# A placement budget with longer step durations and a reserve, in a two-block transformer kernel on one core

## The reference, cut to what matters

```python
def conformer_conv(val_b, gate_b, conv_w, conv_b, ln_g, ln_b):
    g = val_b * jax.nn.sigmoid(gate_b)
    c = causal_depthwise_conv(g, conv_w)      # width CONV_W = 31
    c = c + conv_b
    c = layer_norm(c.reshape(bsz, seq, H_B, HD_B), ln_g, ln_b)   # groups of 128 channels
    return jax.nn.silu(c).reshape(bsz, seq, D_B)                 # D_B = 512

def second_block(...):
    h = rms_norm(x, norm1_g); u_a, v_a, val_b, gate_b = split(h @ w_in)
    mix = concatenate([spatial_gating(u_a, v_a, ...), conformer_conv(val_b, gate_b, ...)])
    x = x + mix @ w_out
    h = rms_norm(x, norm2_g)
    x = x + square(relu(h @ w_ff1)) @ w_ff2
    return rms_norm(x, final_g)
```

## Time and profile before

| what | value |
|---|---|
| median of 3 runs | 2759.99 us |
| the profiled execution | 2761.34 us |
| its span, first to last instruction | 2759.7 us |
| TensorE matmul busy | 2632.9 us (95%) |
| VectorE busy | 1561.2 us (57%) |
| ScalarE busy | 1060.4 us (38%) |
| mean granted TensorE clock | 0.975 |

### The profile page before, as it was taken

One profiled execution on the slowest core, in us unless ns is written; L12 is line 12 of the kernel. 1 busy time (PEld: TensorE's weight loads), 2 busy tenths in 40 slices (PEclk: granted clock), 3 DMA queues, 4 the chain that ended last, 5 costly groups with the idle time before them and its releaser, 6 DMA issues.

```text
span 2759.7 us, 33118 instructions
## 1 busy us (share of the span) xinstructions
PE 2632.9 (95%) x12696; PEld 2164.5 (78%) x12696; DVE 1561.2 (57%) x2392; ACT 1060.4 (38%) x1602; POOL 156.2 (6%) x189
## 2 busy tenths in 40 slices
PE   6999979999899999999999999988999999999997
PEld 5878767777777878888878888876888788888886
DVE  4123325555553666666565895456488854755555
ACT  3123323333432453444554444344434333433332
POOL 1000011111220000110000000000000000000000
PEclk9999988999999999999999999999999999999999
DMA  5222230100103445556553456442322333333331
GB/s 193 94 77 87 75 113 16 39 27 27 39 16 107 131 157 192 192 193 203 192 168 92 145 183 191 132 127 69 101 86 89 92 100 92 92 122 99 92 106 62
DMA packets 318304, 304.29 MB, mean 110 GB/s; under 512 B 10207, under 2 KB 277588, under 8 KB 318036
## 3 DMA queue, kind: packets, MB, share of 16 engines
q1 hardware_dynamic: 303188, 244.18, 29.7%
q0 software_dynamic: 14976, 58.20, 5.2%
HBM read 244.68 MB, written 57.67 MB: 110 GB/s over the span
## 4 chain that ended last, share of the span: by engine, by line
PE 84%; DVE 8%; ACT 3%; DMA 2%; issue 2%; SPq 0%; POOLq 0%; POOL 0%; DVEq 0%; ACTq 0%
PE PS L1854 12%; PE PS L1856 12%; PE PS L1855 12%; PE PS L1568 11%; PE PS L1678 7%; PE PS L1871 6%; PE PS L1872 6%; PE PS L1873 6%; PE PS L1786 3%; PE PS L1809 2%; PE PS L1797 1%; DVE wl L1125 1%; ACT wh L796 1%; DVE cg L1515 1%; DMA raw<-in_w_ff 1%
## 5 line engine op out<-in xcount | busy, mean ns | idle before, releaser
L1854 PE MATMUL PS<-hh,wh 128*128 128x512 f32 x1728 | 683.9, 396 | 4.2 <-DVEq L529 2.3
L1856 PE MATMUL PS<-hh,wl 128*128 128x512 f32 x1728 | 673.9, 390 | 0.0
L1855 PE MATMUL PS<-hl,wh 128*128 128x512 f32 x1728 | 673.6, 390 | 0.0
L1125 DVE TENSOR_TENSOR wl<-raw,wh 128x1024 fp32r<-128x1024 f32 x286 | 347.5, 1227 | 393.6 <-ACT wh L796 393.1
L796 ACT ACTIVATE wh<-raw 128x1024 fp32r<-128x1024 f32 x352 | 366.8, 1055 | 517.7 <-PE PS L1873 381.9
L1411 DVE TENSOR_TENSOR x<-x,PS 128x512 f32<-128x512 f32 x432 | 293.0, 684 | 182.7 <-PE PS L1873 181.8
L1854 PEld LDWEIGHTS PS<-hh,wh 128*128 128x128 f32 x1728 | 325.1, 188 | 76.7 <-issue 4.6
L1855 PEld LDWEIGHTS PS<-hl,wh 128*128 128x128 f32 x1728 | 325.2, 188 | 70.9 <-issue 4.6
L1856 PEld LDWEIGHTS PS<-hh,wl 128*128 128x128 f32 x1728 | 325.0, 188 | 68.2
L1871 PE MATMUL PS<-fh,wh 128*128 128x512 f32 x864 | 344.6, 399 | 18.8 <-DVE x L1411 11.0
L1872 PE MATMUL PS<-fl,wh 128*128 128x512 f32 x864 | 340.0, 393 | 0.0
(11 more groups left out here) (290 smaller groups left out, 2921.2 us busy)
## 6 DMA issues: line engine op xcount, KB each, us to landing
raw<-in_w_ff SPq DMA_DIRECT2D x128, 512.0 KB, 3.9
raw<-in_w_up SPq DMA_DIRECT2D x88, 512.0 KB, 4.4
wl_s<-wl POOLq DMA_DIRECT2D x66, 512.0 KB, 5.5
wl<-wl_s SPq DMA_DIRECT2D x66, 512.0 KB, 3.5
raw<-in_w_in SPq DMA_DIRECT2D x60, 512.0 KB, 3.9
raw<-in_w_down SPq DMA_DIRECT2D x44, 512.0 KB, 5.2
raw<-in_w_out SPq DMA_DIRECT2D x32, 512.0 KB, 4.2
qkvz_s<-st POOLq DMA_DIRECT2D x16, 512.0 KB, 2.9
```

The source lines that it names most:

```text
L1125: TTo(wls(slot), raw[:, k % 2], whs(slot).bitcast(F32), ALU.subtract).then_inc(s["w_lo"], 1)
L1854: mm(bank, wh[:, k % 4, cut], hh[:, kk, span(a_)], start=kk == 0, stop=False)
L1855: mm(bank, wh[:, k % 4, cut], hl[:, kk, span(a_)], start=False, stop=False)
L1856: last = mm(bank, wl[:, k % 4, cut], hh[:, kk, span(a_)], start=False, stop=kk == KT - 1)
```

## The change

`VECTOR_US` now has its own durations for taps, `gate`, `up`, `two`, `ax` and `fx` (0.76 us instead of the 0.66 us of `PASS_US`), `prep` goes from 1.28 to 1.24 and `unit` from 0.45 to 0.5. `PASS_US`, which holds for all other named steps (x additions, `fin`, `low`, `acc`, `al`, the steps of `convs` that aren't listed), goes from 0.66 to 0.70. `background` subtracts a reserve of 0.4 us from the time it may fill. The loop over taps still tests with `PASS_US`, while `put` then counts 0.76. No instruction is added or removed; only the order of the list changes.

```diff
-VECTOR_US = {"prep": 1.28, "high": 0, "unit": 0.45, "cdiag": 0.8, "diag": 0.8, "cols": 0.15, "cvar": 0.15, "mean": 0.15, "var": 0.15,
+VECTOR_US = {"prep": 1.24, "high": 0, "unit": 0.5, "cdiag": 0.8, "diag": 0.8, "cols": 0.15, "cvar": 0.15, "mean": 0.15, "var": 0.15,
              "inv": 0.15, "fcols": 0.15, "finv": 0.15, "fturn": 1.25, "spread": 0, "sq": 0, "turn": 0, "dev": 0, "sig": 0,
-             "v": 0, "silu": 0, "ffn2": 0, "fin2": 0, "mhi": 0}
-UNIT_US, GROUP_US, PASS_US = 5.44, 1.36, 0.66
+             "v": 0, "silu": 0, "ffn2": 0, "fin2": 0, "mhi": 0, "gate": 0.76, "up": 0.76, "two": 0.76, "tap": 0.76, "ax": 0.76,
+             "fx": 0.76}
+UNIT_US, GROUP_US, PASS_US, SPARE_US = 5.44, 1.36, 0.7, 0.4
...
     def background(self, until):
+        until -= SPARE_US
         for chain in (self.norms, self.gating, self.convs):
             while chain and chain[0] != "|" and self.vector_us + VECTOR_US.get(chain[0][0], PASS_US) <= until:
                 self.put(*chain.pop(0))
```

## The result

The changed kernel took 2813.59 us (three runs, 2812.76 to 2813.67; one further execution took 4244.10 us at a mean granted clock of 0.587 and is left out), the kernel before, run beside it, 2760.18. The ratio is 1.0198, 95% interval 1.0178 to 1.0218: slower by 53 us. The forecast was 2810 us, between 2793 and 2830. The profiled execution took 2813.67 us.

A forecast was written before the change was run, and what follows sets the result against it. The prediction took TensorE's work plus its standstills, the largest waiting for VectorE, to bound the kernel. Costs of 71.4 us less 21.3 coming back gave +50 on 2760.0: 2810 us, range 2793 to 2830.

The forecast's parts named there:

- B: Deadline before `out 2 0 0`: 15 taps and the norms of groups 2 and 3 left, costing 22.6 us net.
- E: Deadline before `out 2 1 0`: 25 taps, then two whole norms left, costing 31.9 us net.
- Rivals 2 and 4: Dearer chains at B and E, 2825 us, chance 0.09; B and E hidden beside last groups, 2755.6 us, chance 0.02.
- A: Deadline before `v 0 0`: 7 `ax`/`al` steps left (0 before), costing 2.7 us.
- C: Deadline before `ffn2 0 0`: 12 `ax`/`al` steps left (3 before), costing 6.1 us plus 1.5 for the clock.
- D: Deadline before `v 1 0`: 8 `ax`/`al` steps left (0 before), costing 3.3 us.
- F: Deadline before `ffn2 1 0`: 8 `ax`/`al` steps left (0 before), costing 3.3 us.
- rival 1: Low clock everywhere: restarts behind A, D and F too and a whole one at C, 2818 us, chance 0.12.
- rival 3: More comes back from TensorE's old waits, 38 us instead of 21: 2793 us, chance 0.07.
- S1: Stage from the first inner tile to unit `v 0 0`, holding A: forecast 6.4 us less than before.
- S2: Stage from `v 0 0` to the 20th inner tile, taps of the first half: forecast 5.6 us less.
- S5: Stage from `v 1 0` to the 28th `ffn2`, taps of the second half: forecast 9.7 us less.

The follow-up runs named there:

- e9: The kernel before with all its constants, but no step ever put between the groups of a down pair: 2787.19 us.
- e8: The changed kernel with 0.5 us more to fill ahead of a group, so one step fits between two groups again: 2775.81 us.
- e6: The kernel before with the 0.4 us reserve ahead of units only, unused time not carried over, `cols` and `cvar` held out of groups: 2743.19 us.
- e5: The changed kernel with 170 extra matmuls filling TensorE's waits, 67 at B and 103 at E: 2807.78 us.

## Why the prediction was right

**The leftovers.** The list left what the forecast said: 15 taps in one run at B, 25 at E, as the rows show. Nothing started ahead of the last group: the x addition and `prep` stand in front, 2.56 us to the first step at B for the 2.6 forecast.

**B and E.** B held TensorE for 27.7 us instead of 25.9 (from 1756.71 to 1784.45, one slow start of 0.43 ahead of the unit's second matmul), E for 36.4 instead of 35.2 (2295.67 to 2332.1, read in the same way). The run of 25 taps took 18.40 us, and 10 x 0.66 + 15 x 0.79 is 18.45. What was short, 1.8 and 1.2 us, is mainly one price that stands twice in each chain: I took the pair of small matmuls at 0.87 us from the earlier trace rows, where the granted clock was 1.00, while behind so long a wait it took 2.07 at 0.50. I had priced the low clock for the eight small ones and not for the pair. The restart was too dear by about as much. These are the first starts of the unit behind B, 0.23 us apart from there on:

```profile
1784.88 0.63 PE L1857 MATMUL PS<-hl,wh 128*128 128x512 f32 x1
1785.31 0.54 PE L1858 MATMUL PS<-hh,wl 128*128 128x512 f32 x1
1785.68 0.39 PE L1856 MATMUL PS<-hh,wh 128*128 128x512 f32 x1
```

Reckoned from 1784.45, the third row comes 1.23 us later instead of 0.68, so the restart cost 0.6 us and not 2.3; behind E, in the same way, 1.4 (the tenth start at 2335.60, 3.5 us behind 2332.1 instead of 2.0). In the ledger, B is 28.3 for 28.2, E 38.0 for 37.5. That the two agree so closely is luck: the waits are sized right within 2 us, and at B a pair too cheap and a restart too dear cancel. Rivals 2 and 4 fall with that: the chains were no dearer than 1 to 2 us, and VectorE was not ahead.

**A, C, D, F.** D waited 1.87 + 1.05 = 2.9 us (forecast 3.3), F the same, A 1.09 + 1.08 = 2.2 (2.7). C waited 5.08 us, but the kernel before waited there too:

```profile
1869.27 0.50 PE L1854 MATMUL PS<-hh,wh 128*128 128x512 f32 x1 [1.68 <-DVE hl L1384]
```

So the nine more steps made 3.4 us of wait for the 6.1 forecast, and the clock at 0.50 behind it took 3.0 for the 1.5 (thirteen starts in 5.97 us, from 1888.95 to 1894.92, for 2.95 at 0.227 each). Together C is 6.4 for 7.6. With B and E from the ledger less their 5.6 us of small matmuls, the costs sum to 69.5 us for 71.4. The sum was sized right, though not each of its terms.

**The clock, rival 1.** Behind D and F the granted clock stayed at 1.00 (windows 1982 to 1986 and 2428 to 2432), so low clock everywhere did not come. The forecast's reason against it, that no single gap of the four would be as long as 2.62 us, was wrong for C (5.08). The page's rule (the Trainium skill, "TensorE: Matmul & The Clock Gate", section "The HAM clock gate": throttled by default, released by activity) agrees with the trace at C, where the clock was 0.50 behind the 5.08 us (windows 1888 to 1892 and 1890 to 1894), and decided nothing at D and F, whose two gaps each were 1.9 us at most.

**What comes back.** It was forecast at 21.3 us. By the ledger it was some 16 (69.5 of costs less 53.1), so rival 3 didn't come either. Of its parts these came: 1017 is gone; 2182 is gone; 1896 has gone over into 2.85 us at 1921 (forecast 3.1); 1850 keeps 4.72 of 6.00 (forecast 4.9). Here are the longest stalls of TensorE's timeline that remained in block one, those of A, B and D left out:

```profile
1401.93 1.05 PE L1885 MATMUL PS<-ones,nacc 128*128 128x1 f32 x8 [2.24 <-DVE nacc L1439]
...
1450.16 0.50 PE L1873 MATMUL PS<-fh,wh 128*128 128x512 f32 x1 [2.38 <-DVE x L1413]
...
1868.73 0.76 PE L1873 MATMUL PS<-fh,wh 128*128 128x512 f32 x1 [4.72 <-DVE fl L1433]
...
1888.95 0.80 PE L1856 MATMUL PS<-hh,wh 128*128 128x512 f32 x1 [5.08 <-DVE hl L1386]
...
1921.32 0.50 PE L1873 MATMUL PS<-fh,wh 128*128 128x512 f32 x1 [2.85 <-DVE x L1413]
```

**The step that was off** is the sum of what comes back in block one. S1 was to give back 6.4 us and cost 1.4. The first two of these rows make most of it. The `cols` at 1401 waited 2.24 us. In the kernel before it waited 0.71, which the forecast took back:

```profile
1398.42 1.05 PE L1883 MATMUL PS<-ones,nacc 128*128 128x1 f32 x8 [0.71 <-DVE nacc L1437]
```

The last `fx` and their sums no longer fit between groups, so three sums were put right ahead of it. The x addition at 1450 was 2.38 late, a wait that the forecast doesn't have: `ax` and `al` that no longer fit between groups had been put ahead of the units right before that pair. Each was followed by a low clock (0.66 and 0.64 over the next 4 us, some 1.4 lost each time). That is 2.2 + 2.4 + 2.8 = 7.4 of the 7.8. The step behind it is the forecast's view that waits for x additions come from steps between the groups, so that 5.5 us of them go with these steps. e9 has no such step and waits 12.3 us for x additions, 11.0 before; at 1384 and 1838 it waits 0.98 and 1.73 where the kernel before waited 1.00 and 1.71. What is put ahead of the units makes them as well. The tap stretches went the other way: S2 and S5 gave back 5 us more than forecast (20.3 for 15.3), part of it probably the relief that I had put at nothing. The two misses nearly cancel, which is luck, and why the total is only 3 us off; the forecast's size is better founded at B and E than in its give-backs.

**What I had said of VectorE** was wrong in size: it is 13% less busy in the tap stretch (99.1 for 114.2), not a quarter. The x addition line fell to 6.4 us, not to 1 or 2, for the new stall at 1450, that at 1921 and one of 0.95 stand in it. And E's stall of 18 to 19 us under one run of taps came as 9.16 and 10.88, since `cmean` runs in between.

## What to carry to other kernels

A budget that places side work is a set of thresholds, and what a constant does shows only when the list is written out: here 0.03 us in one duration empties 81 of 84 slots and costs 27 us, while the reserve of 0.4 us ahead of units alone costs nothing on the whole. Before turning such a constant, count per kind of slot how many steps fit and what is left at each deadline, and price the leftovers serially: lead, steps in dependence, the chain, a restart. In this kernel a safer budget needs the room between short entries, and even with it the changed kernel was 16 us slower (e8); a limit on carried-over time (e6), together with the held entries, took out waits that longer durations only moved.

## What the runs showed of the hardware that was not expected

- The pair of 128 x 512 fp32 matmuls behind a norm took 1.02 to 1.12 us at a granted clock of 1.00 and 1.91 to 2.08 at 0.50, as the timelines of e5 and of the changed kernel (its windows 1764 to 1784 and 2304 to 2324) show side by side. The pair whose 0.87 the forecast took from the chain of the earlier trace rows has 1.02 in the timeline, at 1.00.
- Filling a wait with matmuls kept the granted clock at 1.00 through B (28 us), and brought 3 us there: the clock was not the bulk of that stall's cost. A restart has no one price: it cost 2.3 us behind the 4.37 us of the earlier trace rows, 3.0 behind the 5.08 at C, 1.4 behind E and 0.6 behind B.
- Stalls of 2.24, 2.38 and 2.85 us were followed by a granted clock of 0.66, 0.64 and 0.57 over four microseconds (windows 1402 to 1406, 1450 to 1454 and 1922 to 1926); behind 1.87 and 1.05 us it stayed at 1.00.
- Taps of one group in a row take 0.79 us from start to start, taps that alternate between two groups 0.66: 11.77 us for fifteen, 18.40 for ten and fifteen, 13.10 for the seventeen of e9.
